# Two hybrid blocks of two layers each: block one's attention by feature, turns three units behind the scores, a fourth home for weights, and seven reordered places

## The reference

```python
def first_block(...):            # twice
    h = rmsnorm(x, norm_mix[l])
    proj = h @ w_in[l]           # 1024 -> 3476
    y_m = mlstm(...)             # 4 heads of 128: chunked recurrence, normed, gated
    y_b = moba(...)              # 4 heads of 64: causal softmax attention at this length
    y_n = nsa(...)               # 4 heads of 64: g0*compressed + g1*selected + g2*window
    x = x + concat(y_m, y_b, y_n) @ w_out[l]
    h = rmsnorm(x, norm_ffn[l])
    x = x + square(relu(h @ w_ff1[l])) @ w_ff2[l]     # 1024 -> 4096 -> 1024

def second_block(...):           # twice
    p = rms_norm(x, pre_norm[l]) @ w_in[l]            # 1024 -> 6152
    ya = diff_attention(...)     # 4 heads: softmax - lambda * softmax, normed, gated
    yb = stick_breaking(...)     # 8 heads
    yc = forgetting_attention(...)  # 8 heads, "fox"
    x = x + rms_norm(concat(ya, yb, yc) @ w_out[l], post_norm[l])
```

## Time and profile before

| | us |
|---|---|
| median of 3 runs | 1078.39 |
| lowest, highest | 1077.92, 1080.02 |
| the profiled execution | 1078.86 |
| its span, first to last instruction | 1076.7 |
| TensorE busy | 1058.3 (98%) |
| VectorE busy | 762.1 (71%) |
| ScalarE busy | 618.2 (57%) |
| GpSimd busy | 77.8 (7%) |
| mean granted TensorE clock | 0.998 |

### The profile page before, as it was taken

The page is one execution under the profiler, slowest core; times in us unless marked ns, Lnnn a source line. Parts: engine busy times, 40 slices in busy tenths (PEclk is TensorE's granted clock), DMA queues, the critical chain, the costliest instruction groups (busy, mean ns, idle before and its releaser), DMA issues.

```text
span 1076.7 us, 16741 instructions
## 1 busy us (share of the span) xinstructions
PE 1058.3 (98%) x6364; PEld 902.9 (84%) x6364; DVE 762.1 (71%) x1329; ACT 618.2 (57%) x1039; POOL 77.8 (7%) x96
## 2 busy tenths in 40 slices
PE   8999999999999999999999999999999999999997
PEld 7888878888888998888888888798988777989886
DVE  5789777677667889777676666777765667777564
ACT  6676754434446767654344435665757557657572
POOL 1010110000000110110000000003002000030120
PEclk9999999999999999999999999999999999999999
DMA  9853355664666634355556655554453455544531
GB/s 322 269 157 118 92 176 189 189 194 158 203 205 198 199 99 137 100 176 194 187 167 194 206 187 176 159 156 128 146 159 126 147 176 177 156 136 122 174 130 67
DMA packets 89404, 179.04 MB, mean 166 GB/s; under 512 B 8989, under 2 KB 20637, under 8 KB 89325
## 3 DMA queue, kind: packets, MB, share of 16 engines
q1 hardware_dynamic: 88605, 176.58, 52.2%
q10 hardware_dynamic: 720, 1.40, 0.4%
HBM read 176.90 MB, written 1.05 MB: 165 GB/s over the span
## 4 chain that ended last, share of the span: by engine, by line
PE 84%; DVE 7%; ACT 3%; issue 2%; DMA 2%; SPq 1%; POOL 0%; DVEq 0%; POOLq 0%; ACTq 0%
PE bank L859 19%; PE bank L861 19%; PE bank L860 18%; PE bank L925 11%; PE bank L927 5%; PE bank L1013 2%; DVE w_lo L1834 2%; DMA raw<-in_w_in 2%; PE bank L962 2%; PE bank L1070 1%; PE bank L1047 1%; PE bank L1089 1%; PE bank L1088 1%; PE bank L1036 1%; ACT w_hi L1415 1%
## 5 line engine op out<-in xcount | busy, mean ns | idle before, releaser
L1834 DVE TENSOR_TENSOR w_lo<-raw,w_hi 128x1024 fp32r<-128x1024 f32 (+1 forms) x319 | 388.7, 1232 | 176.6 <-ACT w_hi L1415 174.7
L1415 ACT ACTIVATE w_hi<-raw 128x1024 fp32r<-128x1024 f32 (+1 forms) x319 | 330.8, 1052 | 185.0 <-PE bank L861 98.0
L925 PE MATMUL bank<-h_parts,w_hi 128*128 128x512 f32 x512 | 182.0, 399 | 0.3
L859 PE MATMUL bank<-h_parts,w_hi 128*128 128x256 f32 x512 | 149.3, 292 | 1.0 <-DVE w_lo L1834 1.0
L861 PE MATMUL bank<-h_parts,w_lo 128*128 128x256 f32 x512 | 144.7, 283 | 0.0
L860 PE MATMUL bank<-h_parts,w_hi 128*128 128x256 f32 x512 | 144.7, 283 | 0.0
L927 PE MATMUL bank<-h_parts,w_lo 128*128 128x256 f32 x512 | 143.7, 281 | 0.0
L859 PE MATMUL bank<-w_hi,h_parts 128*128 128x512 f32 (+1 forms) x352 | 140.7, 400 | 2.9 <-DVE w_lo L1876 1.5
L861 PE MATMUL bank<-w_hi,h_parts 128*128 128x512 f32 (+1 forms) x352 | 136.0, 386 | 0.0
L860 PE MATMUL bank<-w_lo,h_parts 128*128 128x512 f32 (+1 forms) x352 | 135.9, 386 | 0.0
L925 PEld LDWEIGHTS bank<-h_parts,w_hi 128*128 128x128 f32 x512 | 96.2, 188 | 24.9 <-issue 1.3
(11 more groups left out here) (298 smaller groups left out, 1529.3 us busy)
## 6 DMA issues: line engine op xcount, KB each, us to landing
raw<-in_w_in SPq DMA_DIRECT2D x143, 512.0 KB, 4.2
raw<-in_w_ff SPq DMA_DIRECT2D x128, 512.0 KB, 4.3
raw<-in_w_out SPq DMA_DIRECT2D x40, 512.0 KB, 3.4
raw<-in_w_in SPq DMA_DIRECT2D x8, 404.0 KB, 5.5
xn<-in_cmp_w SPq DMA_DIRECT2D x8, 256.0 KB, 5.5
x_sb<-in_x SPq DMA_DIRECT2D x2, 512.0 KB, 9.0
mix<-in_cmp_w SPq DMA_DIRECT2D x4, 256.0 KB, 4.0
gain<-in_cmp_w SPq DMA_DIRECT2D x4, 256.0 KB, 5.6
```

The costliest lines, as they stand in the source:

```text
L859: pe.matmul(out_ap, s_hi, m_hi, start=start, stop=False, **kw)
L925: pe.matmul(ps[:, :].rearrange("p (a t) -> p a t", a=2), hi[:, kk, f], h_parts[:, :, k, :], start=k == 0, stop=False, skip_group_check=True)
L1415: act.activation(slot(w_hi, u), slot(raw, u), ACT.Copy).then_inc(hi_ready, 1)
L1834: dve.tensor_tensor(slot(w_lo, u), slot(raw, u), slot(w_hi, u).bitcast(F32), ALU.subtract)\
```

## The change

The diff has one large part and several small ones.

- **Heads by feature.** `BY_FEATURE` also names `att1`, the heads of block one. A new step N stands at the end of unit start[h] for each even h: VectorE inverts the pair's row sums (times the gate, from head 4 on), and GpSimd scales the weights of both heads. T stands three units after a head's start instead of two. V goes by pairs, four units after the start of the odd head. Heads 4 to 11 accumulate in one bank (group 1), and `cmp_o` adds into it, so it no longer has its own bank and its own addition. Groups 0 and 1 are read out by ScalarE and VectorE straight into the turned mix (`turned`), at V of heads 3 and 11. `epilogue1` and `mix_turn` 2 and 3 are gone.
- **A fourth home** for weights, for h % 4 = 3: `mix[:, 0, 512:896]`.
- **Orders.** In `heads1` V, E, T, S; the same in block two, where fox gets V, E, N, T, S.
- **Tails.** The last accumulator is registered two units earlier, so that its readers split two units less before they take it, and the last norm turn is registered one unit before the list's end.
- **mlstm's end.** m_values 3 and `mlstm_end(1, 0)` move to p = 29, `mlstm_end(1, 1)` to p = 30. The copy of a head's values moves from ScalarE to VectorE, after the squares.
- **Proj tile.** Four units instead of three on the first half of the tokens; the second half's turns stand after three of them.
- **ff1(1)** puts its fourth bank on 4 instead of 3.
- **forget_log.** The dot products for lambda stand at its start.

```diff
-BY_FEATURE = ("fox",)
+BY_FEATURE = ("att1", "fox",)
@@ tail
-            at_unit[(*name, "acc", a)] = first + 1 if c < 3 else len(units)
+            at_unit[(*name, "acc", a)] = first + 1
@@
             norm_turn(n, order[2] // 2, order[2] % 2)
+            at_unit[steps[-1]] = first + 2
@@ heads1
-            for stage, lag in (("V", 4), ("T", 2), ("E", 1), ("S", 0)):
-                for h in range(12):
-                    if stage == "V" and h > 8:
-                        lag = 3
+            for stage, lag in (("V", 4), ("E", 1), ("T", 3), ("S", 0)):
+                for h in range(stage == "V", 12, 2 if stage == "V" else 1):
@@ units of the projection
-                if p == 25:
-                    single(2, "mix_turn", 0, l, 2)
-                    single(3, "cmp_o", l)
+                    step("cmp_o", l)
+                for h in range(0, 12, 2):
+                    if start[h] == p:
+                        head_steps(("att1", l), h, "N", 4)
@@ units of w_out
-                single(7, "mix_turn", 0, l, 3)
                 m_values(0, 6)
                 m_values(1, 4)
                 step("mlstm_end", l, 0, 0)
                 m_values(2, 5)
+                step("mlstm_end", l, 0, 1)
+            if p == 29:
                 m_values(3, 7)
                 step("mlstm_end", l, 1, 0)
-                step("mlstm_end", l, 0, 1)
-            if p == 29:
+            if p == 30:
                 step("mlstm_end", l, 1, 1)
@@ ff1
-                use(("ff1", l, t, c), ((0, 1, 2, 4), (5, 6, 7, 3))[t][c] if t < 2 else 4 + c)
+                use(("ff1", l, t, c), ((0, 1, 2, 4), (5, 6, 7, 4))[t][c] if t < 2 else 4 + c)
@@ block two
-            for q in range(3):
+            for q in range(4):
                 proj_unit(1, l, w_in_2[l], 0, 0, q, 6144, "vector", place=False)
-        LAGS = {"diff": (("V", 4), ("T", 3), ("C", 2), ("E", 1), ("S", 0)), "fox": (("V", 3), ("T", 2), ("E", 1), ("N", 1), ("S", 0))}
+        LAGS = {"diff": (("V", 4), ("E", 1), ("T", 3), ("C", 2), ("S", 0)), "fox": (("V", 3), ("E", 1), ("N", 1), ("T", 2), ("S", 0))}
@@ homes
+        def weights_home(kind, h):
+            if kind == "att1":
+                return mix[:, 0, 512:896] if h % 4 == 3 else probs[:, h % 4, :]
+            return probs[:, h % 3, :]
@@ TensorE
-                        ps = open_bank(s)
-                        for i in range(NT):
-                            mm = pe.matmul(ps[:, i * T:(i + 1) * T], p_cmpT[:, i, :],
-                                           vc_diag[:, :, :].rearrange("p h d -> p (h d)"), start=True, stop=True)
-                        close(mm, s)
+                        ps = bank[bank_of["att1", l, "O", 1]]
+                        for c in range(2):
+                            pe.matmul(ps[:, c * T:(c + 1) * T], vc_diag[:, 2 * c:2 * c + 2, :].rearrange("p h d -> p (h d)"),
+                                      p_cmpT[:, :, :].rearrange("p i t -> p (i t)"), start=False, stop=False, skip_group_check=True)
@@
-                        for q in range(3):
-                            if i == 0 and q == 2:
+                        for q in range(4):
+                            if i == 0 and q == 3:
                                 for u in range(2):
                                     turn_normed(("norm", 5, 1, u))
@@ ScalarE
-                        link(act.activation(h_num[:, :, h, :], ps[:, 0:258].rearrange("p (i d) -> p i d", i=NT), ACT.Copy))
...
+                                ins.then_inc(h_squared, 1)
+                        if s[2] == "V" and s[3] in (3, 11):
+                            g = s[3] // 8
+                            turned(("att1", l, "O", g), mixT1_hi[1][:, 2 * g:2 * g + 2, :])
@@ GpSimd
+                    elif kind == "att1" and s[2] == "N":
+                        scale_weights("att1", l, s[3])
@@ VectorE
+                        dve.wait_ge(h_squared, MH * l + h + 1)
+                        free(dve.tensor_copy(h_num[:, :, h, :], ps[:, 0:258].rearrange("p (i d) -> p i d", i=NT)), s)
...
-                        elif s[2] == "V" and s[3] % 4 == 3:
-                            epilogue1(s[3] // 4)
+                        elif s[2] == "N":
+                            g, r = divmod(s[3], 4)
+                            gate = n_gate[:, :, s[3]:s[3] + 2].rearrange("p i h -> p h i") if g else None
+                            row_inverses("att1", l, s[3], gate)
+                        elif s[2] == "V" and s[3] in (3, 11):
+                            g = s[3] // 8
+                            turned(("att1", l, "O", g), mixT1_hi[1][:, 2 * g:2 * g + 2, :], mixT1_lo[1][:, 2 * g:2 * g + 2, :])
```

More of the change, by code:

```diff
@@ L458, in hybrid_blocks @@
                     norm_turn(4, 1, 1)
-                if l == 0 or bp or q == 3:
+                if l == 0 or bp:
                     proj_unit(1, l, w_in_2[l], j, bp, q, 6144, "vector")
@@ L1267, in _ @@
                         pair = s[3]
[L1268 to L1273, removed]
+                        pe.wait_ge(mlstm_mixed, 2 * l + pair + 1)
                         turn(s, mix, [(2 * pair + c, i) for c in range(2) for i in range(NT)])
@@ L1277, in _ @@
                         if f % 2 == 0:
-                            drained(pe, ("mix_turn", 0, l, f // 2))
+                            drained(pe, ("att1", l, "O", f // 2 - 2) if f >= 4 else ("mix_turn", 0, l, f // 2))
                         finish_unit(out_unit_products(s, ("out", 0, l), mixT1_hi[f // 4][:, f % 4, :], mixT1_lo[f // 4][:, f % 4, :],
@@ L1321, in _ @@
                                 finish_unit(mm, ("proj", 1, l, 0, q))
+                            elif q == 3:
+                                close(mm, uses_of[0])
                     elif kind == "forget_f":
@@ L1485, in _ @@
                     elif kind == "proj_tile":
-                        split_to(unit_no["proj", 1, l, 0, 2] + s[3])
+                        split_to(unit_no["proj", 1, l, 0, 3] + s[3])
                     if kind == "first_parts":
@@ L2155, in _ @@
                         dve.tensor_tensor(pc, pc, seen_.unsqueeze(2).broadcast_to([P, NT, 4, NC_CMP]), ALU.mult).then_inc(cmp_ready, 1)
-                    elif kind == "cmp_o":
-                        dst = mix[:, :, 768:1024]
-                        free(dve.tensor_tensor(dst, dst, src(s)[:, :].rearrange("p (i c) -> p i c", i=NT), ALU.add), s)
                     elif kind == "mlstm" and s[2] == "S":
@@ L2165, in _ @@
                                                       ALU.mult, ALU.mult), s)
+                    elif kind == "mlstm":
+                        h = s[3]
+                        ps = src(s)
+                        dve.wait_ge(h_squared, MH * l + h + 1)
+                        free(dve.tensor_copy(h_num[:, :, h, :], ps[:, 0:258].rearrange("p (i d) -> p i d", i=NT)), s)
                     elif kind == "att1":
@@ L2277, in _ @@
                     elif kind == "forget_log":
+                        prod = o_tmp[:, 0:2 * HD].rearrange("p (a d) -> p a d", a=2)
+                        lv = lam_v[:, l, :, :].rearrange("p (a b) d -> p a b d", b=2)
+                        tt(prod, lv[:, :, 0, :], lv[:, :, 1, :], ALU.mult)
+                        dve.tensor_reduce(lam[:, 0:2], prod, AX.X, ALU.add).then_inc(lam_dots, 1)
                         f, e = rows[0:8, 2, :], rows[0:8, 1, :]
```

34 lines of the change are left out of this document (7 added, 27 removed).

## The result

| | before | after |
|---|---|---|
| median us | 1078.34 (4 runs) | 1092.15 (4 runs, 1091.1 to 1093.4) |
| ratio | | 1.0122, 95% interval 1.0109 to 1.0134 |
| profiled execution, its span | 1078.86, 1076.7 | 1091.1, 1089.3 |
| mean granted TensorE clock | 0.998 | 0.992 |

The account below looks back on a forecast made before the run. TensorE, busy 98% of the span, was taken to bound the kernel, with VectorE full in stretches of block one. Two layers at +3.75 us, less 1.1 for small places, gave +6.4 and a forecast of 1085.0 us, range 1073 to 1091.

Parts of the forecast that it names:

- (a): TensorE's own work in block one: values by pairs and two turns fewer, -3.3 us a layer.
- (b): Work saved ahead of the `hid` wait is only waited for longer: +1.0 us back a layer.
- (c): The `hid` wait: VectorE's two inversions and contention from three GpSimd scalings make it later, +2.45 us a layer.
- (d): Turns of heads 7 and 9: ScalarE's copies of turned weights come late, +2.75 us a layer.
- (e): End of mlstm: m_values 3 waits 1.85 us for O1's drain while old waits go, +0.85 us a layer.
- Small places: Edits outside block one's heads and mlstm's end, such as tails, fox, dots and proj tile: together -1.1 us.
- The proj tile: Block two, once: turns stand behind the `w_lo` wait, 1.0, and a 0.45 wait for `h_lo` follows: +1.4 us.
- slack absorbs it: Rival, block one: VectorE's delays fall into waits TensorE no longer reaches early; faster, about 1074 us; chance 0.29.
- order alone: Rival, block one: no GpSimd contention but the waits of order stay; no change, about 1078.1 us; chance 0.15.
- Full lock: Rival, block one: each GpSimd scaling costs VectorE its full 0.83 us; slower, about 1088 us; chance 0.14.

Follow-up runs that it names:

- e11: Changed kernel with the proj tile of before, O1 drained before mlstm_end(0,1), and block one's weight scaling moved from GpSimd to ScalarE: 1075.13 us, ratio 0.9971.
- e8: Kernel before with only the tails, block two's orders and forget_log's dots changed: 1074.57 us, ratio 0.9966.
- e12: Changed kernel with the proj tile of before, O1 drained before mlstm_end(0,1), and GpSimd's scaling cut to one column of each block: 1075.24 us, ratio 0.9974.
- e5: Changed kernel with block one's head stages in the order V, T, E, S instead of V, E, T, S: 1090.63 us, ratio 1.0114.
- e3: Changed kernel with TensorE's three longest waits filled by identity turns that nobody reads: 1086.59 us, ratio 1.0072.
- e4: Changed kernel with GpSimd's scaling of block one's weights cut to one column of each 128 x 128 block: 1083.16 us, ratio 1.0044.
- e1: Changed kernel with the proj tile of before, three units with the turns after two: 1086.33 us, ratio 1.0074.

## Why the prediction was wrong

The direction and nearly all mechanisms were right, the size was half.

- **(a), (b).** TensorE's work: right in kind, too large in size. Its busy time fell by 1.2 us only, but the low stretches put about 6 back into it. In e11, with one of them, it is 6.2 below before, but e8, without the layout, is 2.7 below before already. Between e8 and e12, whose small places are the same but for ff1's bank, lie 3.7, or about 5 with e12's early low stretch taken off. Forecast 6.6.
- **(c) `hid`.** Right: 2.5 later in layer 0 against 2.45, and 2.3 in layer 1, where TensorE did wait (1.97). The contention came out as priced there, three scalings at 0.57. Over a layer the twelve cost VectorE 3.9 us, 0.32 each: 0.57, taken from one place where both engines ran large operations, was too much for the average scaling, and the full 0.83 much more so.
- **(d) turns of heads 7 and 9.** Half right. The waits came at the places named, but with 0.90 at head 7 (forecast 2.0) and 0.35 at head 9 (0.75), 1.25 in a layer instead of 2.75; and e5 shows that they are not a price of the order, since VectorE's lateness would have appeared elsewhere. A third wait for `probsT`, 0.59 at head 1, and waits of compression steps (0.8 and up to 1.6) were not forecast.
- **(e) mlstm's end.** The wait was right to 0.2 us. The low clock behind it was left out.
- **Small places.** Each gain came: fox -0.6 twice, `w_lo` -0.6 twice, tails. The proj tile is the mis-sized term: 1.4 forecast, 3.0 without the clock, 4.6 with it. I counted the turns at their 1.0 behind the wait, and missed that the wait, no longer covered by them, becomes 2.88 in one piece.
- **The step that failed** is one that the sum does not have: a wait was priced at its length. Four waits of about 2 us or more each brought 3.4 us of TensorE at half speed, 6.0 us where they lie and 4.2 in the end, and filling the long waits gives 5.6 in e3 (in the traces 0.9 of it is a shorter wait of the compression step L1205, which no fill touches). In the traces the sum goes: 6.4 forecast, + 4.2 clock, + 1.6 proj tile, + 1.1 start of the trace, + 0.1 block one (its layers without the clock cost 3.1 and 3.7, forecast 3.35 each with the tail), - 0.8 the rest of block two: 12.6, as the spans differ. That block one comes out so well is partly luck: too much at the turns of heads 7 and 9 stands against too much saved by (a) and against the waits of head 1 and of the compression, which were not forecast.
- Of the rivals, "slack absorbs it" is refuted by e4, "order alone" too: e4 is what it described, and it lies 9 below. "Full lock" came nearest in time, for the wrong reason.

The layout by feature loses clearly only while GpSimd does the scaling beside a full VectorE. Without that its saved work and its waits of order cancel: e11 and e12 are no faster than e8.

## What to carry to other kernels

Before work is given to an idle GpSimd, look at what VectorE does at that time: if it is full and reads SBUF, the idle engine is not free, and ScalarE can be the better place although it is busier. Where TensorE bounds a kernel, break long waits up, or put work in them: those of 2 us cost up to 1.6 us more than they show. And test several small edits one by one: here three of them were worth 3.8 us and the proj tile lost it all.

## What the runs showed of the hardware that was not expected

- The length of a wait alone does not decide whether the low clock comes: 16 of 27 long waits had it, 6 of 42 shorter ones, and in e1 the same wait of m_values 3 has it in one layer (2.06) and not in the other (2.05). What else decides, these runs do not show.
- GpSimd loses too: the first scaling of each of layer 0's six pairs took 1.72 to 1.74 us, the second 0.82 to 1.81, and none of the kernel's 40 was under 0.82.
- VectorE's copies within SBUF are stretched as its products are: one of 0.23 took 0.51 (at 63.70), beside a product of GpSimd.
